# One hybrid decoder layer on one core: attention levels in pairs, output transposes one slot earlier, one input and two row products later

## The chip, the cores and the metric

The kernel runs on one core of one Trainium2 chip. The metric is the device time of one execution in microseconds (us), as the median of several runs; lower is better.

## The reference

One decoder layer in float32 for 256 tokens of width 2048. Cut to what is computed:

```python
mod = silu(c) @ w_ada + b_ada                 # six rows of 2048: sh1 sc1 gt1 sh2 sc2 gt2
h = rmsnorm(x, g_pre_mix) * (1 + sc1) + sh1
proj = h @ w_in                               # GLA q k v r, low-rank gate, MoBA q k v, gates a, b
log_a = log_sigmoid(ga_low @ w_alpha_up + b_alpha) / 16
o_gla = gla(q * dk**-0.5, k, v, log_a)        # 4 heads, causal, decay exp(b_i - b_j), b = cumsum(log_a)
o_gla = rmsnorm(o_gla, g_head) * silu(gr)
o_moba = causal softmax attention of 8 heads  # 256 tokens are one block
merged = sigmoid(gate_a) * (o_gla @ w_gla_out) + sigmoid(gate_b) * (o_moba @ w_moba_out)
x = x + gt1 * rmsnorm(merged @ w_o, g_post_mix)
h = rmsnorm(x, g_pre_ffn) * (1 + sc2) + sh2
u, g = split(causal_conv3(h @ w_up) + b_conv)
x = x + gt2 * rmsnorm((gelu(g) * u) @ w_down, g_post_ffn)
```

## The kernel before, in words

**Slots.** All large weights stream through one ring of four buffers, `raw`, 1 MB each. A piece of weight, numbered w, has a slot of the program. SyncE loads piece w as soon as `used` counts w - 3, that is when TensorE is through with piece w - 4 (`load_grid`, `load_head`, `load_row`, lines 310 to 340 and 370 to 380). ScalarE rounds it into `hi` (`split_hi`, line 488), VectorE subtracts to get the rest, `lo` (`split_lo`, line 868), and TensorE multiplies: 16 matmuls of 512 columns with `hi`, then as many columns' worth with `lo` (helpers from line 1424 on; all their matmuls carry line 1421). ScalarE and VectorE each work three pieces ahead: in the body of slot w they split piece w + 3. Every engine runs its own list of instructions strictly in the order written.

**Stages.** First 33 slots for the two branch gates and the low-rank gate; then four heads of `HEAD_N` = 12 slots; then 16 merge slots; then 16 slots of `w_o`; then the norm and residual, 22 passes of four slots for `w_up` (`up_pass`), and 44 slots for `w_down`.

**A head.** Head I brings one GLA head and two MoBA heads through the slots n = 0 to 11: n = 0, 1 GLA q and k; 2, 3 MoBA q; 4, 5 MoBA k; 6 to 9 both values; 10, 11 the output gate. Attention of the GLA head with its decay is put together from eight levels of masks. For level p, VectorE makes exponents (`level_decay`, two instructions into `eb`), ScalarE takes exp (line 640), VectorE multiplies q and k with them into `Mb` (`level_operands`), TensorE multiplies these (`gram`, one matmul of 128 x 128 in full float32, which the profile shows as two records), and VectorE copies what the level's mask picks out of PSUM into `C` or `A` (`select`). Before the change one level goes through in each of the slots 3 to 10: `gram` is called behind the weights of the slot, and all other steps are spread over the neighbouring slots. `eb` and `Mb` have two buffers, used in turn by even and odd levels.

**Between heads.** Behind slot 11 TensorE forms the head's output (`A` times values, into bank 4). ScalarE squares it and takes a root, VectorE the reciprocal (line 1158). Then, in slot 0 of the next head, ScalarE first splits piece w + 3 and only then scales the output into `ot` (`token_major`, line 592):

```python
                    split_hi(w + 3)
                    if I and n == 0:
                        token_major(I - 1)
                    if I:
                        tail(I - 1, n)
```

TensorE's `tail(prev, n)` does the rest behind the weights of the next head's slots: transposes of the softmax weights `ssb` in slot 0 (line 1601), of `ot` in slot 1 (line 1607; it waits for `ot_done`), the MoBA value products in slot 2. For the last head these lie in the merge slots 0, 0 and 2, and there `token_major` stands ahead of the split.

**Rows of c @ w_ada.** GpSimd loads 128 pieces of 512 KB of `w_ada` (line 474), VectorE accumulates them (`ada_unit`, lines 892, 897), so many in each slot as `UNITS_3`, `UNITS_H`, `UNITS_L` and `UNITS_M` say. The gain row `G1` (`g_post_mix` on all partitions, 1 MB) is loaded by GpSimd behind 96 of them (line 460) once `g_done` counts 2, and multiplied in `w_o` slots 4 and 5 (line 1214).

**Residual.** `x2`, the 2 MB of x for the residual, is loaded by SyncE in the loop over `w_o`, behind the load of piece kt = 4 (line 376); first read by line 747, behind the last split of that stage.

**Sums in the up stage.** In passes 8 and 17 VectorE and ScalarE bring a finished row sum into `asp`, and TensorE adds it up over the partitions with `ones_r`, behind the fourth slot of the same pass, where it waits for `g_lo` (four matmuls of 512 columns). `gate_row` reads the result in the third slot of passes 9 and 18.

Of the kernel before, what the change touches and what calls it, by code (L numbers as in the profile page):

```python
# [12 lines left out]
P = 128  # L13
# [3 lines left out]
def layer_kernel(nc, x, c, w_ada, b_ada, g_pre_mix, w_in, w_alpha_up, b_alpha, g_gla_head, w_gla_out,  # L17
# [70 lines left out]
    UNITS_3 = {25: 1, 26: 1, 27: 1, 28: 2, 29: 2, 30: 2, 31: 2, 32: 1}  # L88
    UNITS_H = [2, 1, 1, 1, 1, 1, 1, 2, 2, 2, 2, 2]
    UNITS_L = [2, 1, 1, 1, 1, 1, 1, 2, 2, 1, 0, 0]  # L90
    UNITS_M = [1, 1, 2, 1, 0, 2, 0, 2, 1, 2, 0, 2, 1, 1, 0, 1]
# [22 lines left out]
    with ctx:  # L114
# [169 lines left out]
        UP_FIRST = (0, 2, 1, 3)  # L284

        def score_cols(qt):
            return slice(0, P) if qt == 0 else slice(P, 3 * P)
# [17 lines left out]
        def _(sp):  # L305
# [65 lines left out]
            for kt in range(KT):  # L371
                sp.wait_ge(used, W_WO + kt - 3)
                load_row(W_WO + kt, wo, kt)
                if kt == 4:
                    sp.wait_ge(oo_ready, 4)
                    sp.dma_start(x2[:, :, :], x_v).then_inc(xr_in, 16)
# [29 lines left out]
        def _(pool):  # L406
# [45 lines left out]
            for u in range(8 * KT):  # L452
                part, t = divmod(u, KT)
                if u == 4 * KT - 2:
                    bias_row(4, acc_a)
                if u == 5 * KT - 2:
                    bias_row(5, acc_b)
                if u == 6 * KT:
                    pool.wait_ge(g_done, 2)
                    pool.dma_start(G1[:, :], g_post_mix[0].partition_broadcast(P)).then_inc(g1_in, 16)  # L460
                if u == 6 * KT + 2:
                    bias_row(6, acc_a)
                    pool.wait_ge(arr[W_UP % 4], fills(W_UP))
                    pool.wait_ge(x2_ready, 6)
                    pool.tensor_copy(hi[:, W_UP % 4, :], raw[:, W_UP % 4, :]).then_inc(hi_done, 1)
                    pool.wait_ge(h2_ready, 8)
                    pool.dma_start(G2[:, :], g_post_ffn[0].partition_broadcast(P)).then_inc(g2_in, 16)
                if u == 7 * KT + 2:
                    bias_row(7, acc_a)
                if u == WIDE_FROM:  # L470
                    pool.wait_ge(tri_done, 1)
                if last_in_slot(u) >= 0:
                    pool.wait_ge(ada_used, last_in_slot(u) + 1)
                pool.dma_start(unit_buffer(u), wada[:, t, PART_COL[part]:PART_COL[part] + 1024]).then_inc(ada_in[unit_slot(u)], 16)  # L474
# [3 lines left out]
        def _(act):  # L478
# [96 lines left out]
            def tail(prev, n):  # L575
                if n == 0:
# [4 lines left out]
                    act.activation(tg[:, :, :], grt[:, :, :], ACT.Tanh, scale=0.5).then_inc(tanh_done, 1)  # L581
                if n == 2:
                    t = om_tile(2 * prev)
# [14 lines left out]
            for I in range(HEADS):  # L598
                for n in range(HEAD_N):
# [32 lines left out]
                    if n in (6, 8):  # L632
                        act.wait_ge(mod_done, 4 + I + 1)
                        for j in range(2 * n - 12, 2 * n - 8):
                            part = ps[:, 6 + j // 4, P * (j % 4):P * (j % 4 + 1)]
                            col = M_SH2 * KT + 8 * I + j
                            act.activation(part, part, ACT.Identity, accum_out=modsf[:, col:col + 1]).then_inc(part_read, 1)
                    for p in ((0, 1) if n == 0 else (n,) if 2 <= n <= 7 else ()):
                        act.wait_ge(e_ready, 8 * I + p + 1)
                        act.activation(eb[:, p % 2, :], eb[:, p % 2, :], ACT.Exp).then_inc(exp_done, 1)  # L640
# [207 lines left out]
        def _(dve):  # L848
# [208 lines left out]
            def before_select(I, lv):  # L1057
                if lv:
                    dve.wait_ge(select_done, 8 * I + lv)
                dve.wait_ge(gram_done, 9 * I + (1 if lv == 0 else lv + 2))  # L1060

            def select(I, lv):
# [4 lines left out]
                if lv == 1:  # L1067
                    dve.wait_ge(a_done, I + 1)
                dve.copy_predicated(C[:, :], mask8[:, lv, :], ps[:, 4 if lv % 2 else 5, 0:P]).then_inc(select_done, 1)
                if lv == 7:  # L1070
# [26 lines left out]
            for I in range(HEADS):  # L1097
                for n in range(HEAD_N):
# [21 lines left out]
                    if n == 2:  # L1120
                        a_zero = link(dve.memset(A[:, 0:3:2, :], 0.0), wait=False)
                    if 3 <= n <= 10:
                        if n == 3:
                            linked(a_zero)
                        before_select(I, max(n - 3, 0))
                        if n - 1 <= 7:
                            level_operands(I, n - 1)
                        if n == 10:
                            dve.wait_ge(p_ready, 4 * I + 4)
                            link(dve.reciprocal(stat[:, 28:32], stat[:, 24:28]), wait=False)  # L1130
                        select(I, n - 3)
                    if 2 <= n <= 7:
                        level_decay(I, n)
                    if n == HEAD_N - 1 and I == HEADS - 1:
# [68 lines left out]
            for kt in range(KT - 3):  # L1203
# [3 lines left out]
                if kt == 2:  # L1207
                    dve.wait_ge(g_done, 1)
                    zero_acc(6)
                if kt in (4, 5):  # L1210
                    cs = slice(1024 * (kt - 4), 1024 * (kt - 3))
                    dve.wait_ge(g_copied, kt - 3)
                    dve.wait_ge(g1_in, 16)
                    dve.tensor_tensor(G1[:, cs], gsum[:, cs], G1[:, cs], ALU.mult).then_inc(g_ready, 1)
                    dve.tensor_copy(ones_r[:, :], ones[:, :])
                if kt == 4:
# [202 lines left out]
        def _(pe):  # L1419
# [158 lines left out]
            def gram(I, p):  # L1578
                bank = 4 if p % 2 else 5
                pe.wait_ge(level_ready, 8 * I + p + 1)  # L1580
                if p == 0:
                    if I:
                        pe.wait_ge(og_f, I)
                    mm(ps[:, 5, 0:P], Mb[:, 0, 0:P], Mb[:, 0, P:]).then_inc(gram_done, 1)
                    return
                if p == 2:
                    pe.wait_ge(a01_done, I + 1)
                else:
                    pe.wait_ge(select_done, 8 * I + max(p - 1, 1))
                mm(ps[:, bank, 0:P], Mb[:, p % 2, 0:P], Mb[:, p % 2, P:]).then_inc(gram_done, 1)  # L1590

# [4 lines left out]
            def tail(prev, n):  # L1596
                if n == 0:
                    for hd in range(2):
# [3 lines left out]
                        ins.then_inc(pt_done, 1)  # L1602
                if n == (1 if prev < HEADS - 1 else 0):
                    pe.wait_ge(ot_done, 2 * prev + 2)
# [3 lines left out]
                    ins.then_inc(ott_done, 1)  # L1608
                if n == 2:
                    for hd in range(2):  # L1610
# [5 lines left out]
            for I in range(HEADS):  # L1616
                for n in range(HEAD_N):
# [18 lines left out]
                    if n == 3:  # L1636
# [4 lines left out]
                        ins.then_inc(gram_done, 1)  # L1641
                    if 3 <= n <= 10:
                        gram(I, n - 3)
                    if n == 5:
                        if I:
# [116 lines left out]
            def up_pass(i, sums=None, order=range(4)):  # L1762
                for p_, n in enumerate(order):
                    g = n // 2
                    if n % 2 == 0:
# [3 lines left out]
                                  None if order == range(4) else h2_is_ready).then_inc(used, 1)  # L1769
                    if sums is not None and n == 3:  # L1770
                        pe.wait_ge(g_lo, sums - 5)
# [6 lines left out]
            up_pass(0, order=UP_FIRST)  # L1778
            with pe.Fori(1, 8) as i:
                up_pass(i)  # L1780
            up_pass(8, 6)
            with pe.Fori(9, 17) as i:
                up_pass(i)
            up_pass(17, 7)
            with pe.Fori(18, UP_ITERS) as i:
                up_pass(i)
# [46 lines left out]
```

## Time and profile before

| | us |
|---|---|
| median of 3 runs | 1461.57 (1461.25 to 1464.21) |
| the profiled execution | 1462.59 |
| its span, first to last instruction | 1460.9 |
| TensorE busy with matmuls | 1428.0 (98%) |
| TensorE busy loading weights | 1215.0 (83%) |
| VectorE busy | 1094.6 (75%) |
| ScalarE busy | 721.0 (49%) |
| chain that ended last | TensorE 86%, VectorE 5%, DMA 4% |

How to read it: matmuls are pipelined, so what a group costs TensorE is the distance from its first start to the first start of the next group, not the duration printed. A timeline row gives the start, the time from the first start to the last end, the engine, the line, the operation, the tiles, the shape, how many instructions are merged, and in brackets the idle time before them and what ended it. Times are from the start of the span.

### The profile page before, as it was taken

The numbers are of one execution on the slowest core, as the hardware profiler recorded it, in microseconds if no ns is written. First come the engines' busy times: TensorE is split into PE (matmuls) and PEld (weight loads), VectorE is DVE, ScalarE is ACT, GpSimd is POOL, SyncE is SP. The second block draws the span as 40 slices with busy tenths as digits, with TensorE's granted clock in tenths as the row PEclk, the third lists the DMA queues.
The fourth block names the chain that finished last, engine by engine and source line by source line (L and its number), as shares of the span: only waits on it lengthen the run. The fifth ranks groups of instructions, "written<-read, shape, count | busy, mean of one in ns | idle before, by whom it ended". The sixth has DMA issues, their size and how long they took to land.

```text
span 1460.9 us, 19754 instructions
## 1 busy us (share of the span) xinstructions
PE 1428.0 (98%) x7322; PEld 1215.0 (83%) x7322; DVE 1094.6 (75%) x1145; ACT 721.0 (49%) x820; POOL 84.6 (6%) x165
## 2 busy tenths in 40 slices
PE   4999999999999999999999999999999999999998
PEld 3788888888888888878888888888888888888886
DVE  6899989898989888845787787777777766545545
ACT  5454354554545466333855554454455455443443
POOL 2000011111111100000000000000000000000000
PEclk9999999999999999999999999999999999999999
DMA  9999979898989877865477776677675655555553
GB/s 361 387 387 385 308 252 371 288 311 277 315 271 299 272 246 250 293 264 201 135 254 239 236 243 222 199 241 239 222 243 174 200 180 195 195 191 189 201 189 128
DMA packets 235833, 367.07 MB, mean 251 GB/s; under 512 B 11503, under 2 KB 161521, under 8 KB 235010
## 3 DMA queue, kind: packets, MB, share of 16 engines
q1 hardware_dynamic: 215840, 294.69, 60.5%
q0 software_dynamic: 18848, 69.23, 13.1%
q10 hardware_dynamic: 1090, 2.40, 0.4%
q8 instruction: 36, 0.59, 0.2%
q14 instruction: 19, 0.16, 0.0%
HBM read 364.18 MB, written 2.10 MB: 251 GB/s over the span
## 4 chain that ended last, share of the span: by engine, by line
PE 86%; DVE 5%; DMA 4%; issue 2%; ACT 2%; SPq 0%; DVEq 0%
PE ps L1421 85%; DVE acc L878 2%; DMA raw<-in_w_in 1%; DMA raw<-in_w_o 1%; DMA adar<-in_w_ada 1%; DVE lo L868 1%; DMA raw<-in_w_up 1%; DMA raw<-in_w_moba_out 1%; ACT hi L488 1%; DVE GA L998 0%; ACT hi L812 0%; DVE lo L1369 0%; DVE yt L1241 0%; PE ps L1671 0%; DVE x L1244 0%
## 5 line engine op out<-in xcount | busy, mean ns | idle before, releaser
L1421 PE MATMUL ps<-hT,hi 128*128 128x512 f32 x1936 | 465.8, 392 | 0.8 <-DVE hT L1266 0.8
L1421 PEld LDWEIGHTS ps<-hT,hi 128*128 128x128 f32 x1936 | 356.1, 188 | 71.6 <-DVE hT L1266 1.1
L488 ACT ACTIVATE hi<-raw 128x2048 fp32r<-128x2048 f32 x115 | 220.3, 1917 | 278.4 <-DMA raw<-in_w_in 190.2
L868 DVE TENSOR_TENSOR lo<-raw,hi 128x2048 fp32r<-128x2048 f32 x115 | 262.7, 2286 | 79.2 <-ACT hi L488 78.9
L1421 PEld LDWEIGHTS ps<-hT,lo 128*128 128x128 f32 x1920 | 246.1, 191 | 9.8 <-DVE lo L868 0.5
L1421 PE MATMUL ps<-hT,lo 128*128 128x256 f32 x1920 | 249.1, 283 | 0.1
L1369 DVE TENSOR_TENSOR lo<-raw,hi 128x2048 fp32r<-128x2048 f32 x88 | 199.2, 2290 | 36.8 <-ACT hi L812 36.6
L1421 PE MATMUL ps<-hi,hT 128*128 128x512 f32 x768 | 186.2, 394 | 0.2 <-DVE GA L998 0.2
L1421 PE MATMUL ps<-hi,asp 128*128 128x512 f32 x704 | 175.8, 389 | 0.0
L812 ACT ACTIVATE hi<-raw 128x2048 fp32r<-128x2048 f32 x88 | 165.8, 1906 | 14.0 <-DMA raw<-in_w_up 12.6
L1421 PEld LDWEIGHTS ps<-hi,hT 128*128 128x128 f32 x768 | 142.5, 188 | 32.3 <-issue 1.4
L1421 PEld LDWEIGHTS ps<-hi,asp 128*128 128x128 f32 x704 | 132.1, 188 | 27.4
L1400 DVE TENSOR_TENSOR lo<-raw,hi 128x2048 fp32r<-128x2048 f32 x40 | 91.7, 2292 | 49.5 <-ACT hi L834 49.5
L474 POOL DMA_DIRECT2D ada<-in_w_ada x128 | 67.7, 530 | 688.5 <-DVE acc_a L1338 295.0
L1421 PE MATMUL ps<-lo,asp 128*128 128x512 f32 x352 | 96.1, 389 | 0.0
L1421 PE MATMUL ps<-lo,hT 128*128 128x512 f32 x384 | 95.0, 389 | 0.0
L790 ACT ACTIVATE cv<-ps 128x512 f32<-128x512 f32 x44 | 26.4, 600 | 125.0 <-PE ps L1421 125.0
L1421 PEld LDWEIGHTS ps<-lo,hT 128*128 128x128 f32 x384 | 72.1, 188 | 15.0
L878 DVE SCALAR_TENSOR_TENSOR acc<-adar,scol,acc 128x1024 f32<-128x1024 f32 x59 | 75.7, 1282 | 11.1 <-DMA adar<-in_w_ada 7.1
L801 ACT ACTIVATE asp<-aT 128x256 fp32r (+1 forms) x44 | 18.0, 416 | 124.7 <-PE ps L1421 124.7
L794 ACT ACTIVATE cv<-up,cols 128x256 f32<-128x256 f32 x88 | 48.2, 595 | 61.5 <-DVE up L1351 61.5
L1421 PEld LDWEIGHTS ps<-lo,asp 128*128 128x128 f32 x352 | 66.0, 188 | 14.0 <-DVE lo L868 0.3
(257 smaller groups left out, 1296.4 us busy)
## 6 DMA issues: line engine op xcount, KB each, us to landing
raw<-in_w_up SPq DMA_DIRECT2D x176, 512.0 KB, 4.5
raw<-in_w_in SPq DMA_DIRECT2D x161, 512.0 KB, 6.0
ada<-in_w_ada POOLq DMA_DIRECT2D x128, 512.0 KB, 5.2
raw<-in_w_down SPq DMA_DIRECT2D x88, 512.0 KB, 4.2
adar<-in_w_ada SPq DMA_DIRECT2D x64, 512.0 KB, 11.0
raw<-in_w_o SPq DMA_DIRECT2D x32, 512.0 KB, 4.9
raw<-in_w_gla_out SPq DMA_DIRECT2D x16, 512.0 KB, 4.9
raw<-in_w_moba_out SPq DMA_DIRECT2D x16, 512.0 KB, 5.8
```

Source lines behind the costliest of these rows:

```text
L474: pool.dma_start(unit_buffer(u), wada[:, t, PART_COL[part]:PART_COL[part] + 1024]).then_inc(ada_in[unit_slot(u)], 16)
L488: act.activation(hi[:, w % 4, :], raw[:, w % 4, :], ACT.Copy).then_inc(hi_done, 1)
L790: act.activation(cv[:, :, :], ps[:, 2 * g:2 * g + 2, TOK:], ACT.Copy).then_inc(cross5, 1)
L794: act.activation(cv[:, ct, :], up[:, ct, 2:], ACT.Identity, scale=cols[:, ds(f + COL_CONV + 4 * FT, 1)], bias=cols[:, ds(f + COL_CB, 1)]). ...
L801: act.activation(asp[:, k, 0:TOK], aT[:, ds(kt, 1), :], ACT.Copy).then_inc(a_hi, 1)
L812: act.activation(hi[:, w % 4, :], raw[:, w % 4, :], ACT.Copy).then_inc(hi_done, 1)
L868: dve.tensor_tensor(lo[:, w % 4, :], raw[:, w % 4, :], hi[:, w % 4, :].bitcast(F32), ALU.subtract).then_inc(lo_done, 1)
L878: ins = dve.scalar_tensor_tensor(a, adar[:, u % 8, :], scol[:, t:t + 1], a, ALU.mult, ALU.add)
L1369: dve.tensor_tensor(lo[:, k, :], raw[:, k, :], hi[:, k, :].bitcast(F32), ALU.subtract).then_inc(lo_done, 1)
L1400: dve.tensor_tensor(lo[:, k, :], raw[:, k, :], hi[:, k, :].bitcast(F32), ALU.subtract).then_inc(lo_done, 1)
L1421: return pe.matmul(out_, lhsT, rhs, start=start, stop=stop)
```

## The change

- Levels in pairs: `gram` is called twice behind each of the slots 3, 5, 7 and 9, and VectorE's selects and operands, and ScalarE's exponentials, go in pairs. `level_place` gives each level of a pair its own columns of PSUM. `UNITS_H` and `UNITS_L` move `ada_unit` calls from slots 3 and 5 to 4 and 6.
- The transposes of `ot` stand in slot 0 of the next head in all heads; the MoBA value products in slot 3.
- `x2` is loaded behind piece kt = 9, `G1` once `used` counts `W_WO + 6`; its product is in `w_o` slots 9 and 10, and `ones_r` is written in slot 2.
- The sums of the up stage stand behind the first slot of passes 9 and 18.

```diff
-    UNITS_H = [2, 1, 1, 1, 1, 1, 1, 2, 2, 2, 2, 2]
-    UNITS_L = [2, 1, 1, 1, 1, 1, 1, 2, 2, 1, 0, 0]
+    UNITS_H = [2, 1, 1, 0, 2, 0, 2, 2, 2, 2, 2, 2]
+    UNITS_L = [2, 1, 1, 0, 2, 0, 2, 2, 2, 1, 0, 0]
...
+        def level_place(p):
+            if p < 2:
+                return (4, slice(2 * P, 3 * P)) if p else (5, slice(0, P))
+            return (4 if p // 2 == 2 else 5), slice(P * (p % 2), P * (p % 2 + 1))
...
-                if kt == 4:
+                if kt == 9:
                     sp.wait_ge(oo_ready, 4)
                     sp.dma_start(x2[:, :, :], x_v).then_inc(xr_in, 16)
...
                 if u == 6 * KT:
-                    pool.wait_ge(g_done, 2)
+                    pool.wait_ge(used, W_WO + 6)
                     pool.dma_start(G1[:, :], g_post_mix[0].partition_broadcast(P)).then_inc(g1_in, 16)
...
-                if n == 2:
+                if n == (3 if prev < HEADS - 1 else 2):
                     t = om_tile(2 * prev)
...
-                    for p in ((0, 1) if n == 0 else (n,) if 2 <= n <= 7 else ()):
+                    for p in ((n, n + 1) if n in (0, 2, 4, 6) else ()):
...
-                    if 3 <= n <= 10:
+                    if n in (3, 5, 7, 9):
                         if n == 3:
                             linked(a_zero)
-                        before_select(I, max(n - 3, 0))
-                        if n - 1 <= 7:
+                        before_select(I, n - 3)
+                        if n < 9:
                             level_operands(I, n - 1)
-                        if n == 10:
-                            dve.wait_ge(p_ready, 4 * I + 4)
-                            link(dve.reciprocal(stat[:, 28:32], stat[:, 24:28]), wait=False)
+                            level_operands(I, n)
                         select(I, n - 3)
-                    if 2 <= n <= 7:
-                        level_decay(I, n)
+                        before_select(I, n - 2)
+                        select(I, n - 2)
+                    if n == 10:
+                        dve.wait_ge(p_ready, 4 * I + 4)
+                        link(dve.reciprocal(stat[:, 28:32], stat[:, 24:28]), wait=False)
+                    if n in (2, 3, 5):
+                        p = {2: 2, 3: 4, 5: 6}[n]
+                        level_decay(I, p)
+                        level_decay(I, p + 1)
...
+                    dve.tensor_copy(ones_r[:, :], ones[:, :])
-                if kt in (4, 5):
-                    cs = slice(1024 * (kt - 4), 1024 * (kt - 3))
-                    dve.wait_ge(g_copied, kt - 3)
+                if kt in (9, 10):
+                    cs = slice(1024 * (kt - 9), 1024 * (kt - 8))
+                    dve.wait_ge(g_copied, kt - 8)
                     dve.wait_ge(g1_in, 16)
                     dve.tensor_tensor(G1[:, cs], gsum[:, cs], G1[:, cs], ALU.mult).then_inc(g_ready, 1)
-                    dve.tensor_copy(ones_r[:, :], ones[:, :])
...
             def gram(I, p):
-                bank = 4 if p % 2 else 5
+                bank, cs = level_place(p)
                 pe.wait_ge(level_ready, 8 * I + p + 1)
...
-                if n == (1 if prev < HEADS - 1 else 0):
+                if n == 0:
                     pe.wait_ge(ot_done, 2 * prev + 2)
...
-                if n == 2:
+                if n == (3 if prev < HEADS - 1 else 2):
                     for hd in range(2):
...
-                    if 3 <= n <= 10:
+                    if n in (3, 5, 7, 9):
                         gram(I, n - 3)
+                        gram(I, n - 2)
...
-                    if sums is not None and n == 3:
+                    if sums is not None and n == 0:
                         pe.wait_ge(g_lo, sums - 5)
...
-            up_pass(8, 6)
+            up_pass(9, 6)
...
-            up_pass(17, 7)
+            up_pass(18, 7)
```

## Rows read from the trace of the kernel before

**Rows 1.** The page, part 1: TensorE's matmuls.

```profile
PE 1428.0 (98%) x7322; PEld 1215.0 (83%) x7322; DVE 1094.6 (75%) x1145; ACT 721.0 (49%) x820; POOL 84.6 (6%) x165
```

**Rows 2.** TensorE's waits: who for whom, us in total, times, longest.

```profile
PE ps L1476 <- DMA rows<-in_b_conv: 16.5, 1, 16.5
```

**Rows 3.** Timeline of TensorE in the w_o stage, kt = 3 to 6.

```profile
637.41 1.98 PE L1421 MATMUL ps<-hi,mT 128*128 128x512 f32 x8
...
650.66 2.11 PE L1421 MATMUL ps<-hi,mT 128*128 128x512 f32 x8 [1.44 <-ACT hi L488]
...
656.75 0.61 PE L1421 MATMUL ps<-hi,mT 128*128 128x512 f32 x2
```

**Rows 4.** The tile x: time from issue to landing of its one load.

```profile
DMA to landing us min/median/max: 13.0/13.0/13.0
```

**Rows 5.** Timeline of TensorE at the end of up pass 8.

```profile
919.84 2.07 PE L1421 MATMUL ps<-hT,lo 128*128 128x256 f32 x16
922.74 1.19 PE L1421 MATMUL ps<-asp,ones_r 128*128 128x512 f32 x4 [0.83 <-DVE asp L1374]
```

**Rows 6.** Timeline of TensorE in head 0: slot 7, and behind slot 9's weights.

```profile
268.63 3.92 PE L1421 MATMUL ps<-hi,hT 128*128 128x512 f32 x16
...
274.34 3.92 PE L1421 MATMUL ps<-hi,hT 128*128 128x512 f32 x16
...
285.63 0.38 PE L1421 MATMUL ps<-Mb 128*128 128x128 f32 x2
285.85 1.48 PE L1421 MATMUL ps<-mqk 128*128 128x128 f32 x8
```

**Rows 7.** Timeline of TensorE in the merge stage: a slot with weights alone.

```profile
605.82 3.79 PE L1421 MATMUL ps<-hi,og_om 128*128 128x512 f32 x16
...
611.26 1.07 PE L1421 MATMUL ps<-hi,og_om 128*128 128x512 f32 x4
```

**Rows 8.** Timeline of TensorE, slot 0 of head 1 to the start of slot 1.

```profile
303.49 2.08 PE L1421 MATMUL ps<-hT,lo 128*128 128x256 f32 x16
305.40 0.82 PE L1601 MATMUL ps<-ident,ssb 128*128 128x128 f32 x6
305.97 3.92 PE L1421 MATMUL ps<-hT,hi 128*128 128x512 f32 x16
```

**Rows 9.** Timeline of ScalarE in the same stretch.

```profile
305.01 1.92 ACT L488 ACTIVATE hi<-raw 128x2048 fp32r<-128x2048 f32 x1 [1.56 <-DMA raw<-in_w_in]
306.83 0.82 ACT L592 ACTIVATE ot<-ps,stat 128x256 f32<-128x256 f32 x2
```

**Rows 10.** Timelines, heads 2 and 3: TensorE's start of slot 1, ScalarE's scaling.

```profile
380.64 3.92 PE L1421 MATMUL ps<-hT,hi 128*128 128x512 f32 x16
...
381.56 0.82 ACT L592 ACTIVATE ot<-ps,stat 128x256 f32<-128x256 f32 x2
...
455.32 3.92 PE L1421 MATMUL ps<-hT,hi 128*128 128x512 f32 x16
...
456.88 0.82 ACT L592 ACTIVATE ot<-ps,stat 128x256 f32<-128x256 f32 x2
```

**Rows 11.** Issues by SyncE, and the split that waited for the second load's landing.

```profile
298.71 0.92 SPq L307 DMA_DIRECT2D raw<-in_w_in  x2
...
656.94 0.81 SPq L307 DMA_DIRECT2D raw<-in_w_o  x2
...
661.75 1.93 ACT L488 ACTIVATE hi<-raw 128x2048 fp32r<-128x2048 f32 x1 [2.57 <-DMA raw<-in_w_o]
```

**Rows 12.** The tile G (instructions), and VectorE's timeline late in the w_o stage.

```profile
L1214 DVE TENSOR_TENSOR G<-gsum,G x2: 1218/1218/1219, 658.9 to 662.7; 128x1024 f32<-128x1024 f32 x2
...
680.50 2.29 DVE L868 TENSOR_TENSOR lo<-raw,hi 128x2048 fp32r<-128x2048 f32 x1 [3.67 <-ACT hi L488]
```

**Rows 13.** Stretches: length, busy time of five engines, granted clock, DMA share, GB/s.

```profile
32.00:40.00 8.00, 8.00 (x31) 5.01 (x32) 6.58 (x13) 3.84 (x5) 0.00 (x0) 0.79 1.05 387
648.00:651.00 3.00, 1.56 (x8) 0.98 (x6) 0.36 (x1) 1.91 (x1) 0.00 (x0) 1.00 1.02 401
```

More of the change, by code:

```diff
@@ L1059, in before_select @@
                     dve.wait_ge(select_done, 8 * I + lv)
-                dve.wait_ge(gram_done, 9 * I + (1 if lv == 0 else lv + 2))
+                dve.wait_ge(gram_done, 9 * I + (lv | 1) + 2)
             def select(I, lv):
@@ L1068, in select @@
                     dve.wait_ge(a_done, I + 1)
-                dve.copy_predicated(C[:, :], mask8[:, lv, :], ps[:, 4 if lv % 2 else 5, 0:P]).then_inc(select_done, 1)
+                bank, cs = level_place(lv)
+                dve.copy_predicated(C[:, :], mask8[:, lv, :], ps[:, bank, cs]).then_inc(select_done, 1)
                 if lv == 7:
@@ L1578, in gram @@
             def gram(I, p):
-                bank = 4 if p % 2 else 5
+                bank, cs = level_place(p)
                 pe.wait_ge(level_ready, 8 * I + p + 1)
[L1581 to L1586, printed above, removed]
+                if p == 0 and I:
+                    pe.wait_ge(og_f, I)
+                if p in (2, 3):
                     pe.wait_ge(a01_done, I + 1)
-                else:
-                    pe.wait_ge(select_done, 8 * I + max(p - 1, 1))
-                mm(ps[:, bank, 0:P], Mb[:, p % 2, 0:P], Mb[:, p % 2, P:]).then_inc(gram_done, 1)
+                if p >= 4:
+                    pe.wait_ge(select_done, 8 * I + (2 if p < 6 else 4))
+                mm(ps[:, bank, cs], Mb[:, p % 2, 0:P], Mb[:, p % 2, P:]).then_inc(gram_done, 1)
             def causal_product(out_, values, weights):
@@ L1778, in _ @@
             up_pass(0, order=UP_FIRST)
-            with pe.Fori(1, 8) as i:
+            with pe.Fori(1, 9) as i:
                 up_pass(i)
-            up_pass(8, 6)
-            with pe.Fori(9, 17) as i:
+            up_pass(9, 6)
+            with pe.Fori(10, 18) as i:
                 up_pass(i)
-            up_pass(17, 7)
-            with pe.Fori(18, UP_ITERS) as i:
+            up_pass(18, 7)
+            with pe.Fori(19, UP_ITERS) as i:
                 up_pass(i)
```

## The prediction

> **What bounds the kernel now.** I began with the page: matmuls keep TensorE busy for 98% of the span [rows 1]. So time can only be won where TensorE stands still or does avoidable work, and the change moves no arithmetic away. Next, TensorE's waits: the largest, 16.5 us, is the start, before any code the diff touches [rows 2]. Then I walked TensorE's timeline and compared starts, since a short stall hides under a "busy" engine. One tile of a w_o slot is 12 matmuls at 0.227 us, 2.72 us. From the first tile of kt = 3 to that of kt = 6 are six tiles, 16.32 us, but the rows say 656.75 - 637.41 = 19.34: 3.0 us are lost there, the longest wait of 1.44 us ending with a ScalarE split that had itself waited for a weight [rows 3]. That is where x comes in, 13.0 us from issue to landing [rows 4]. In up pass 8 the 16 `lo` matmuls should end their turn 1.91 us after 919.84 (the same sixteen take that from 303.49 to 305.40 [rows 8]); the sums start at 922.74, 1.0 us late, waiting for `asp` [rows 5]. In the heads there is no such gap: slots follow each other at full rate.
>
> **Part 1, levels in pairs.** The same 32 levels are multiplied; only their company changes. A slot with one level lasts 274.34 - 268.63 = 5.71 us [rows 6], one with weights alone 611.26 - 605.82 = 5.44 [rows 7]: a lone level costs 0.27. Inside a group of full-float32 matmuls the next start comes 0.22 after it [rows 6]. Dissolving a group into another therefore saves at most 0.05, and not less than nothing. Four groups go per head (slots 4, 6, 8, 10), 16 in all; moving the `ot` transposes and the value products dissolves 3 + 3 more. Eight of the 22 lie ahead of slots shaped like the one measured: 0.4 us. The other fourteen are worth 0 to 0.7; I take 0.2. **Saved 0.6 us, bounds 0.4 to 1.1.**
>
> What the pairs move elsewhere costs nothing as long as its cover holds. VectorE now waits in slot 3 for both levels, with an evacuation and a split queued behind; ScalarE's exponentials of a pair stand behind the split of slots 2, 4 and 6. But splits are three pieces ahead of TensorE, some 17 us at 5.71 a slot, and a pair adds only a few small instructions to VectorE's turn. In slots 4, 6, 8 and 10 it no longer waits for a level at all, which is where the moved `ada_unit` calls go. The sum of the calls is unchanged, as is their number in slots 7 to 11, so GpSimd's loads around the head boundary stay as they are.
>
> **Part 2, output transposes in slot 0.** This is the part that costs. The wait for `ot_done` now stands ahead of all of slot 1's matmuls. Before, TensorE begins slot 1 of head 1 at 305.97, right behind the `ssb` transposes [rows 8]; that is where it would now begin on `ot`. But ScalarE has `ot` ready at 306.83 + 0.82 = 307.65 [rows 9]. Stall: 1.7 us. In head 2: 381.56 + 0.82 - 380.64 = 1.7. In head 3: 456.88 + 0.82 - 455.32 = 2.4 [rows 10]. The last head's transposes already stood in merge slot 0 and do not move. **Sum 5.8 us, all on the path**, as TensorE has nothing else in its queue.
>
> Can ScalarE be earlier? Its scaling stands behind a split that it starts at 305.01, after 1.56 us idle, waiting for the load of piece w + 3 [rows 9]. SyncE could issue that load only when slot 11 was through, 298.71; landing took 6.3 us [rows 11]. The change leaves all of this as it is. The nearest row for a faster landing is a w_o weight with the DMA queues otherwise quiet: issued 656.94, split begun 661.75, 4.8 us [rows 11]. Everything would be 1.5 us earlier, and that is all of ScalarE's idle time (1.56): stalls of 0.2, 0.2 and 0.9, 1.3 in all. For a slower one, the nearest is head 3's own 2.4 in all three heads: 7.1. I take 5.8, since contention at that moment comes from the same neighbours.
>
> **Part 3, x and the post-mix row later.** With no 2 MB of x and no 1 MB row (and no two units behind it in GpSimd's queue) between them, the loads of kt = 4 to 7 come as a quiet load does, 4.8 us, and are split 1.92 later; TensorE wants each over 10 us after its issue. The 3.0 us vanish. They could return later: `used` reaches `W_WO + 6` at about 653.7, and then kt = 9, x, the row and two units are issued together. Taking x at its 13.0 us [rows 4], and half as much again for the 1 MB of kt = 10 behind it in the same queue, that weight lands by 19.5 after the burst, is rounded by 21.4, and TensorE reaches it four slots on, 21.8. So even the slow price fits, by 0.4; a quiet landing (13.0 + 4.8) fits by 2. The row's products, 2 x 1.22 us, now lie in slots 9 and 10, where VectorE idles 3.67 before a split [rows 12]; both results are first read behind this stage. **Saved 3.0 us, bounds 0 and 3.0.**
>
> **Part 4, sums one slot later.** `asp` was 1.0 us late and now has a whole slot more; pass 17 had no such wait. `gate_row` reads two slots later, and VectorE only gets there when TensorE is past the sums. **Saved 1.0 us, bounds 0 and 1.1.**
>
> **Sum:** 5.8 - 0.6 - 3.0 - 1.0 = **+1.2 us** on the profiled execution's own 1462.59. That run was 1.0 above the median of the runs, 1461.57, so on the median's scale I forecast 1461.57 + 1.2 = **1462.8**. No more than 0.2% (2.9 us) can be told from no change here, so this is "same": two repairs of 4 us, eaten by a new wait.
>
> **A rule that speaks against the change.** What rows show first: the one earlier stall of comparable length, at 648 to 651, left the granted clock at 1.00, while from 32 to 40, after a stretch with little matmul work, its mean was 0.79: TensorE was partly at 1.2 GHz, and 8.0 x 0.21 = 1.7 us of work were lost [rows 13]. The Trainium skill (TensorE: Matmul & The Clock Gate, Part 1: The HAM clock gate) has it that an idle TensorE is put back to half rate and has to be busy for a while to get it back. Nothing in the sum rests on it; as a rival it is the second below.
>
> **Rivals.**
> *A, ScalarE arrives sooner* (faster). If the load lands as a quiet one does, stalls shrink to 1.3: -3.3, **1458.3**. For: units were shuffled among the slots. Against: the counts near the boundary are unchanged, and three heads agree within 0.7 us. 12%.
> *B, the clock falls in the new stalls* (slower). Each of three stalls costs another 1.7 of half-rate work: 1.2 + 5.1 = +6.3, **1467.9**. It decides from two heads on (+4.6). By the skill's rule as told above the same would follow wherever a gap counts as idle. Against: the 1.44 us wait with clock 1.00 [rows 3, 13]; for: head 3's is longer. 7%.
> *C, x's stall only moves.* The burst of x, the row and the units is slower than its 13.0 us, and the 3.0 us come back at kt = 10: +4.2, **1465.8**, slower. Against: the margin above. 8%.
> *D, the transposes do not wait*, for instance because work I count as fixed in slot 0 grows anyway: then -4.6, 1457.0. The code excludes it nearly: 2%.
>
> **How the numbers follow.** Forecast case 64%; with its bounds on parts 1 and 2 (+5.8 to between 4.5 and 7.1) it spans 1461.5 to 1464.1, and a median's own scatter some 0.5 more. About 7% is left for things not thought of, mostly slower. Faster by over 0.2%: A, D, 0.14. Same: 0.64. Slower: B, C and the rest, 0.22. The range runs from 1459.0 to 1466.0: it takes in C and the weaker part of A, and leaves out B and the end of A.
>
> **What would show it.** In the changed profile: TensorE idle 1.7, 1.7 and 2.4 us ahead of the `ot` transposes in heads 1 to 3, released by ScalarE's scaling, with clock 1.00; w_o tiles 2.72 apart from kt = 3 to 11, x still landing before the stage ends; no wait on `asp`; eight lone level groups gone in favour of pairs, a pair's slot some 0.45 us over a bare one. I am wrong if that idle is missing or twice as long, or if w_o stalls near kt = 10.

## The result and the profile after

| | us |
|---|---|
| before, median of 16 runs | 1461.74 (1460.52 to 1464.21) |
| changed, median of 16 runs | 1467.05 (1463.19 to 1475.36) |
| ratio | 1.0041, 95% interval 1.0032 to 1.0049 |
| changed, the profiled execution | 1474.32, span 1472.6 |

The change makes the kernel 5.3 us slower, where I had forecast +1.2, called it no change, and given a range of 1459.0 to 1466.0. The profiled execution is one of the slower of its kernel, so its waits are read for their kind and place, and the sizes come from medians.

The page of the changed kernel, part 1, answers [rows 1]: as many matmuls, a longer span.

```profile
PE 1431.5 (97%) x7322; PEld 1219.1 (83%) x7322; DVE 1094.8 (74%) x1144; ACT 720.9 (49%) x820; POOL 83.8 (6%) x165
```

TensorE's waits of the changed kernel. The second line is new; the waits for a `w_o` split and for `asp` of before are gone.

```profile
PE ps L1488 <- DMA rows<-in_b_conv: 16.4, 1, 16.4
PE ps L1616 <- ACT ot L598: 9.6, 3, 3.9
PE ps L1502 <- ACT xn L522: 4.6, 1, 4.6
```

TensorE's timeline at the start of head 1, answering [rows 8]: softmax transposes, the wait, the `ot` transposes (L1616), and then slot 1.

```profile
304.45 2.08 PE L1433 MATMUL ps<-hT,lo 128*128 128x256 f32 x16
306.37 0.81 PE L1610 MATMUL ps<-ident,ssb 128*128 128x128 f32 x6
311.06 1.11 PE L1616 MATMUL ps<-ident,ot 128*128 128x128 f32 x4 [3.88 <-ACT ot L598]
311.83 5.89 PE L1433 MATMUL ps<-hT,hi 128*128 128x512 f32 x16
317.55 1.72 PE L1433 MATMUL ps<-hT,lo 128*128 128x256 f32 x13
```

The place and the releaser are the forecast ones; the size is not. I had read off 1.7 us, here it is 3.9. And the 16 matmuls behind it take 5.89 us where slot 1's took 3.92 before [rows 8].

The bracket prints a little less than TensorE loses. Counted from start to start, the wait is 311.06 - 306.37 - 0.65 = 4.0 us, where 0.65 is what the six softmax transposes take when nothing holds up the next group (305.26 to 305.91 in a run below). In heads 2 and 3 it is 3.1 and 3.0 by the same count, 10.1 in all. Lengths of single waits below are counted in this way; the lines of the waits view print some tenths less.

ScalarE's timeline in the same stretch, answering [rows 9]: its idle time before the split is 3.95 us, not 1.56.

```profile
304.12 0.30 ACT L661 ACTIVATE stat<-stat,eps 128x2 f32<-128x2 f32 x1
308.37 1.91 ACT L494 ACTIVATE hi<-raw 128x2048 fp32r<-128x2048 f32 x1 [3.95 <-DMA raw<-in_w_in]
310.19 0.82 ACT L598 ACTIVATE ot<-ps,stat 128x256 f32<-128x256 f32 x2
```

SyncE's timeline: the load that this split waits for, answering [rows 11]. From its issue to the split it took 308.37 - 299.68 = 8.7 us, against 6.3 before.

```profile
299.68 0.92 SPq L313 DMA_DIRECT2D raw<-in_w_in  x2
```

Stretches of the changed kernel: length, busy time of TensorE's matmuls and weight loads, VectorE, ScalarE, GpSimd, then the granted clock, DMA share, GB/s. The first three each hold the start of one head.

```profile
304.00:322.00 18.00, 14.12 (x73) 12.19 (x72) 12.40 (x19) 8.66 (x14) 2.59 (x5) 0.81 0.83 270
384.00:402.00 18.00, 15.02 (x79) 12.95 (x79) 13.16 (x21) 9.76 (x14) 2.64 (x5) 0.91 0.88 297
463.00:481.00 18.00, 15.21 (x82) 13.23 (x81) 16.08 (x23) 11.23 (x19) 2.11 (x4) 0.91 0.76 246
482.00:1472.00 990.00, 982.14 (x5090) 841.31 (x5088) 685.95 (x685) 490.44 (x526) 34.90 (x63) 1.00 0.65 218
```

Behind all three waits TensorE ran partly at 1.2 instead of 2.4 GHz; from 482 us on it is at full clock. Rival B has happened.

The `w_o` stage, answering [rows 3], from the first tile of kt = 3: tiles 2.72 us apart, no wait.

```profile
653.45 1.98 PE L1433 MATMUL ps<-hi,mT 128*128 128x512 f32 x8
655.26 1.07 PE L1433 MATMUL ps<-lo,mT 128*128 128x512 f32 x4
656.16 1.98 PE L1433 MATMUL ps<-hi,mT 128*128 128x512 f32 x8
```

The load of x now takes 14.2 us, from `DMA to landing us min/median/max: 14.2/14.2/14.2`, 1.2 more than before, and nothing waits for it. The sums of the up stage start 1.91 us after the `lo` group ahead of them, with no wait, answering [rows 5]:

```profile
938.40 2.08 PE L1433 MATMUL ps<-hT,lo 128*128 128x256 f32 x16
940.31 1.09 PE L1433 MATMUL ps<-asp,ones_r 128*128 128x512 f32 x4
```

### The profile page after: what moved, and what is told of

It is laid out like the page before. It is cut to its first block, busy times and chain, and to the rows that moved or that the text cites. A ratio compares the mean times of both kernels' runs of the same rounds, so it can differ in the third digit from the quotient of the medians.

```text
span 1472.6 us, 19749 instructions
## 1 busy us (share of the span) xinstructions
PE 1431.5 (97%) x7322; PEld 1219.1 (83%) x7322; DVE 1094.8 (74%) x1144; ACT 720.9 (49%) x820; POOL 83.8 (6%) x165
## 4 chain that ended last, share of the span: by engine, by line
PE 87%; DMA 5%; DVE 3%; ACT 2%; issue 1%; SPq 1%; DVEq 0%
PE ps L1433 87%; DMA raw<-in_w_in 3%; DVE acc L884 1%; DMA adar<-in_w_ada 1%; ACT hi L494 1%; DMA ada<-in_w_ada 1%; DMA raw<-in_w_moba_out 1%; SPq L313 0%; DVE acc_a L903 0%; DVE lo L874 0%; DVE yt L1253 0%; DVE x L1256 0%; PE ps L1681 0%; PE ps L1616 0%; PE ps L1660 0%
```

## The experiments

All were timed beside the kernel before on the same chip; medians are in us. "Before" was 1461.87, 1462.18, 1461.86 and 1461.96 in the four groups of runs. Sizes of single waits are from one profiled execution each, and single waits differ by 1 us and more between two executions of one kernel.

### What the place of the transposes is worth

**Changed kernel, transposes back in slot 1.**

```diff
-                if n == 0:
+                if n == (1 if prev < HEADS - 1 else 0):
                     pe.wait_ge(ot_done, 2 * prev + 2)
```

> The changed kernel with the output transposes back in slot 1 of the next head. If their wait in slot 0 and the half-rate clock behind it are the whole loss: no wait on ot, granted clock 1.00 in the heads, and the savings of the other parts remain, -4.6 us against the kernel before, about 1457. If the pairs or the moved units disturb VectorE or the loads by themselves: TensorE idles elsewhere in the heads and the time stays at 1461 or above.

Measured: 1458.34, ratio 0.9975 (0.9967 to 0.9984). TensorE's waits have no line for `ot`, and the heads run back to back. So slot 0 costs 1467.05 - 1458.34 = 8.7 us, and the rest of the change saves 3.5, not 4.6. The two medians are from different groups of runs; by the two ratios the price would be 9.6 us, and their intervals allow 7 to 12.

**Kernel before, transposes in slot 0.** The move of the transposes and nothing else.

> The kernel before with the output transposes moved to slot 0 and nothing else. If the loss is this wait alone and it is as long as in the changed kernel (about 10 us in three stalls, plus 1 to 2 us each of half rate): +10 us or more against before, about 1471. If the changed kernel's stalls are longer than the 5.8 us that I read off because the pairs and units delay the load: stalls of about 1.7, 1.7 and 2.4 us here, +6 us, about 1468, and little or no half rate.

Measured: 1468.81, ratio 1.0053 (1.0036 to 1.0069), 6.9 us slower. The profiled execution, 1466.09, is the fastest of its six; its waits are short and its clock in the heads is full:

```profile
PE ps L1607 <- ACT ot L592: 3.9, 3, 1.8
```

The move alone makes the kernel slower. By starts the three waits are 1.2, 2.0 and 1.2 us, 4.4 in all, and this execution is 4.2 above the median of before, 1461.87: waiting accounts for it. The median of 6.9 is nearer to the second theory (+6) than to the first (+10 or more). It is 1.1 above the 5.8 that I had read off, and the six runs have a mean granted clock of 0.9973, where the runs of before in this group have 0.9985: so some half rate seems to occur here too.

### What makes ot late

**Changed kernel, ScalarE scales before it splits.**

```diff
-                    split_hi(w + 3)
                     if I and n == 0:
                         token_major(I - 1)
+                    split_hi(w + 3)
```

> The changed kernel with ScalarE's scaling of ot put ahead of its split of piece w + 3 in slot 0, in all heads. The transposes stay in slot 0. If the stall is the order on ScalarE (scaling behind a split that waits for a load): stalls fall from 3 to 4 us to at most 0.5 us, what is left being VectorE's reciprocal behind its own split; no half rate; about 1458.5. If ot is late for another reason, the stalls stay above 1.5 us.

Measured: 1461.5, ratio 0.999 (0.9982 to 0.9999), 5.6 below the changed kernel. Timeline of head 1, ScalarE and then VectorE: the scaling no longer waits for a load. It waits 2.62 us for the reciprocal, which VectorE makes behind its own split.

```profile
302.97 0.30 ACT L661 ACTIVATE stat<-stat,eps 128x2 f32<-128x2 f32 x1
305.88 0.84 ACT L598 ACTIVATE ot<-ps,stat 128x256 f32<-128x256 f32 x2 [2.62 <-DVE stat L1170]
...
303.49 2.28 DVE L874 TENSOR_TENSOR lo<-raw,hi 128x2048 fp32r<-128x2048 f32 x1
305.69 0.16 DVE L1170 RECIPROCAL stat<-stat 128x2 f32<-128x2 f32 x1
```

The first order explains most of the wait, and a second one lay hidden under it. I had expected at most 0.5 us of it to be left, and 1458.5; that was too little and too fast. TensorE still waits, by starts 0.9, 0.3 and 1.1 us:

```profile
PE ps L1616 <- ACT ot L598: 1.7, 2, 0.9
```

**The same, and VectorE's reciprocal before its split in slot 11.**

```diff
-                    split_lo(w + 3)
                     if n == HEAD_N - 1:
                         dve.wait_ge(root_done, I + 1)
                         dve.reciprocal(stat[:, 14:16], stat[:, 12:14]).then_inc(rr_ready, 1)
+                    split_lo(w + 3)
```

> The changed kernel, transposes in slot 0, with ScalarE's scaling ahead of its split as in the earlier run (1461.5, stalls left of 0.9, 0.3 and 1.1 us that ended with the scaling, which itself waited 2.6 us for VectorE's reciprocal), and now VectorE's reciprocal ahead of its split in slot 11 too. If both orders together made ot late: no stall at slot 0, 1458 to 1459, as with the transposes in slot 1. If something else holds ot up: stalls of 0.3 us or more stay and the time stays near 1461.

Measured: 1458.62, ratio 0.9977 (0.9967 to 0.9986). Head 1, TensorE, then ScalarE and VectorE:

```profile
305.26 0.81 PE L1610 MATMUL ps<-ident,ssb 128*128 128x128 f32 x6
305.91 0.60 PE L1616 MATMUL ps<-ident,ot 128*128 128x128 f32 x4
...
303.54 0.84 ACT L598 ACTIVATE ot<-ps,stat 128x256 f32<-128x256 f32 x2 [0.23 <-DVE stat L1169]
...
303.34 0.17 DVE L1169 RECIPROCAL stat<-stat 128x2 f32<-128x2 f32 x1 [0.43 <-ACT stat L661]
```

`ot` is ready at 304.38, 1.5 us ahead of its use, and in heads 2 and 3 TensorE does not wait for it either; 0.2 us is left in the merge stage, where the transposes stood in slot 0 before too. With both orders turned the move is free within what these runs tell (1458.62 against 1458.34 in slot 1): the place in slot 0 is not the cause, the two producers behind splits are.

### Why the wait was longer than read off

**Changed kernel, unit counts of before.**

```diff
-    UNITS_H = [2, 1, 1, 0, 2, 0, 2, 2, 2, 2, 2, 2]
+    UNITS_H = [2, 1, 1, 1, 1, 1, 1, 2, 2, 2, 2, 2]
```

(`UNITS_L` likewise.)

> The changed kernel with the unit counts of before in slots 3 to 6 (1, 1, 1, 1 in place of 0, 2, 0, 2). If the moved units are what lengthens the landing at the head boundary (8.3 us for the second half of the load in head 1, against 5.9 before): stalls shrink to the 5.8 us in all that I had read off, about 1463. If it is the pairs' timing on VectorE, or contention that comes out differently from run to run: stalls stay near 10 us and the time near 1467.

Measured: 1465.17, ratio 1.0022 (1.0011 to 1.0033), 1.9 below the changed kernel's first median and 2.4 below its second (next section). The interval just touches that of the first and overlaps that of the second, so the size is uncertain. The waits are 1.4, 2.5 and 3.0 us, 6.9 in all: between the 5.8 and the 10 of the two theories. GpSimd's issues of `w_ada` pieces ahead of the load in question (SyncE, 298.71 before, 299.68 changed, 298.73 in this run): the kernel before, the changed one, and this run.

```profile
294.39 0.53 POOL L474 DMA_DIRECT2D ada<-in_w_ada  x1 [5.49 <-DVE acc_b L897]
295.78 0.53 POOL L474 DMA_DIRECT2D ada<-in_w_ada  x1 [0.86 <-DVE acc_b L897]
```

```profile
296.51 0.53 POOL L480 DMA_DIRECT2D ada<-in_w_ada  x1 [6.30 <-DVE acc_b L903]
297.90 0.53 POOL L480 DMA_DIRECT2D ada<-in_w_ada  x1 [0.86 <-DVE acc_b L903]
```

```profile
294.67 0.53 POOL L480 DMA_DIRECT2D ada<-in_w_ada  x1 [6.30 <-DVE acc_b L903]
296.06 0.53 POOL L480 DMA_DIRECT2D ada<-in_w_ada  x1 [0.86 <-DVE acc_b L903]
```

With the counts changed only in slots 3 to 6, VectorE comes to its units of slot 10 later. In head 1 their buffers come free 1.8 and 3.2 us ahead of the load, where it was 2.9 and 4.3; with the old counts it is 2.7 and 4.1 again. The same two distances can be read at the three head boundaries of twelve profiles, those in which neither order was turned and the counts were one of these two sets:

| kernel | boundaries | first piece ahead of the load, mean us | issue to split, us |
|---|---|---|---|
| old counts, single levels | 12 | 4.0 | 5.8 to 7.5, mean 6.4 |
| old counts, pairs | 6 | 3.7 | 5.4 to 7.6, mean 6.5 |
| the change's counts, pairs | 18 | 2.5 | 6.1 to 8.7, mean 7.3 |

So it is the moved units and not the pairs that make the load late, by about 0.8 us a boundary, 2.5 in three: about what this run takes away. That sharing the DMA engines with the 512 KB pieces is the link is argued from these distances; no run shows it by itself. Old counts are not free of long landings either: 7.6 us in head 3 of this run.

**Changed kernel, no units in slots 10 and 11.** Meant to take those pieces out of the way.

```diff
-    UNITS_H = [2, 1, 1, 0, 2, 0, 2, 2, 2, 2, 2, 2]
+    UNITS_H = [2, 1, 1, 2, 2, 2, 2, 2, 2, 2, 0, 0]
```

> The changed kernel with no units in slots 10 and 11 of heads 0 to 2, and two in each of slots 3 to 6 instead (18 a head as before), so that no piece of w_ada is in flight when the load that ScalarE waits for is issued. If sharing the DMA engines with those pieces is what stretches the landing from 6.5 to between 7.8 and 8.9 us behind the output product: landing in 5 us or a little more, three stalls of about 0.3 to 1 us, little half rate, 1459 to 1461. If the landing is long by itself: unchanged, 1467.

Measured: 1476.49, ratio 1.0097 (1.0082 to 1.0112), a miss in both ways. In heads 1 and 2 it did not empty the DMA engines: two units in each of slots 3 to 9 make VectorE so late that a piece is still issued 0.7 us ahead of the load, and the split begins 7.5 and 8.0 us behind the load's issue. In head 3 no piece is issued in the 5.8 us ahead of it, but ScalarE comes to its split late, at 465.77, without waiting for the load, and VectorE's reciprocal begins only at 467.34. So by the old orders `ot` is late all the same:

```profile
PE ps L1616 <- ACT ot L598: 9.9, 3, 4.0
```

So it does not tell what a quiet landing would be. That figure stays open.

### What the clock adds

**The changed kernel again.**

> The changed kernel itself once more, on the same chip as the three others. Its first profile was one of its slowest executions (1474.32 against a median of 1467.05). Expected: median 1466 to 1468, three stalls between 1.5 and 4 us, and half rate behind those over about 2.5 us only, so that stalls and half rate together account for its scatter.

Measured: 1467.54, ratio 1.0035 (1.0023 to 1.0046). Its profiled execution has waits of 2.3, 2.7 and 3.0 us, and half rate behind all three, also behind the one below the 2.5 that I had expected. The clock in the heads:

```profile
304.00:322.00 18.00, 15.82 (x89) 13.89 (x88) 14.81 (x21) 8.56 (x13) 2.42 (x5) 0.91 0.93 313
384.00:402.00 18.00, 15.48 (x86) 13.50 (x85) 14.96 (x21) 8.57 (x13) 2.11 (x4) 0.91 0.85 291
463.00:481.00 18.00, 15.20 (x76) 12.97 (x75) 13.91 (x20) 8.39 (x12) 1.58 (x3) 0.81 0.73 231
```

18 us at means of 0.91, 0.91 and 0.81 are 1.6 + 1.6 + 3.4 = 6.6 us of work at full rate; some of that time was waiting, in which the clock costs nothing. What it costs can be read from starts. The `ot` transposes and the 16 matmuls behind them take 4.1 us at full rate (305.91 to 310.03 in head 1 with both orders turned) and here 5.8, 5.6 and 7.0: 6.0 us lost. With 8.0 of waiting that makes 14.0, and this execution (1472.41) is 14.1 above the kernel with its transposes in slot 1. In the first profile of the changed kernel it is 10.1 of waiting and 2.4 + 1.7 + 1.3 = 5.4 of half rate (in head 1, 317.55 - 311.06 = 6.5 in place of 4.1), 15.5 for 16.0. The two together are the whole loss in both.

**Six matmuls in the wait.** TensorE multiplies the identity with a constant while it waits.

```diff
                 if n == 0:
+                    if prev < HEADS - 1:
+                        for _k in range(6):
+                            mm(ps[:, 5, :], ident[:, :], causal[:, :])
                     pe.wait_ge(ot_done, 2 * prev + 2)
```

> The changed kernel with six extra matmuls of 512 columns (identity times a constant, 0.43 us each, into a bank that the transposes overwrite) between TensorE's softmax transposes and its wait for ot, in heads 1 to 3. It changes no dependency, only what TensorE does while it waits. If half rate behind the stalls comes from TensorE's idleness: the granted clock stays 1.00 in the heads, no matmuls 0.43 us apart behind the transposes, and where the stall is over 2.6 us nothing is lost by the filler: 1 to 3 us less than the changed kernel, 1464 to 1466. If the clock does not matter, the time is the changed kernel's or up to 1 us more per head with a short stall.

Measured: 1474.78, ratio 1.0081 (1.0068 to 1.0094), where I had expected 1464 to 1466. The filler was twice as long as I wrote:

```profile
307.18 5.32 PE L1433 MATMUL ps<-causal,ident 128*128 128x512 f32 x12
312.33 0.60 PE L1619 MATMUL ps<-ident,ot 128*128 128x128 f32 x4
312.69 1.63 PE L1433 MATMUL ps<-hT,hi 128*128 128x512 f32 x6
```

`ot` was always ready first. Three fillers of 5.2 us on the 1458.34 of transposes in slot 1 make 1474, as measured. The clock is whole, although TensorE was kept from its real work for longer than in the changed kernel:

```profile
304.00:322.00 18.00, 18.00 (x90) 13.66 (x89) 14.06 (x21) 8.96 (x14) 2.64 (x5) 1.00 0.91 294
```

**Three matmuls.** The same with `range(3)`.

> As the six-matmul filler, with three. Each of those matmuls in full float32 turned out as two records of 0.43 us, so six took 5.2 us where the stall was 2.3 to 4; three take 2.6. If idleness is what brings half rate: none behind the transposes, idle of at most 1.4 us left in each head, and where the stall exceeds 2.6 us the filler is free: 3 to 4 us less than the changed kernel's 1467.3, 1463.5 to 1465. If half rate costs nothing by itself, or comes anyway: 1467 or more.

Measured: 1467.52, ratio 1.0038 (1.0024 to 1.0051). The granted clock in the heads is 1.00 again, as expected, but no time is won, where I had expected 3 to 4 us. The filler sets a floor of 2.6 us a head, and its profiled execution waits 0.4 more in one head only; that makes about 8.3, against 8.7 for the changed kernel with its clock. Filling the wait removes the half rate and not the loss. That fits a typical execution that loses mostly by waiting, which is argued here and not shown.

How much the clock costs in a typical execution can be estimated from the 16 runs of the changed kernel. Their mean granted clocks average 0.9971, from 0.993 to 0.999, against 0.998 in the profile of before: 0.0009 x 1465 = 1.3 us. Against the 88 runs of before beside the experiments, which average 0.9983, it is 1.8. The clocks are recorded in steps of 0.001, and they count waiting as well, so this is no more than an estimate. The two slowest runs, 1475.36 and 1474.32, have 0.995 and 0.993.

### The other parts alone

**Before with pairs and their unit counts.** The change's edits to levels and units alone.

> The kernel before with the pairs of levels and their unit counts alone; transposes in slot 1, value products in slot 2, x, the row and the sums as before. By my reading: -0.4 to -0.6 us, about 1461.2, TensorE's single-level slots gone. If pairs cost something (VectorE late, longer landings that reach TensorE): slower than before, with idle on TensorE in the heads.

Measured: 1462.43, ratio 1.0005 (0.9996 to 1.0013): no gain. Lone levels' slots of 5.71 us [rows 6] are gone; in the changed kernel a slot with a pair, and the slot after it, read

```profile
269.79 3.79 PE L1433 MATMUL ps<-hi,hT 128*128 128x512 f32 x16
273.42 1.98 PE L1433 MATMUL ps<-lo,hT 128*128 128x512 f32 x8
275.23 0.60 PE L1433 MATMUL ps<-Mb 128*128 128x128 f32 x4
275.60 3.89 PE L1433 MATMUL ps<-hi,hT 128*128 128x512 f32 x16
279.32 1.98 PE L1433 MATMUL ps<-lo,hT 128*128 128x512 f32 x8
281.13 3.79 PE L1433 MATMUL ps<-hi,hT 128*128 128x512 f32 x16
```

5.81 us, of which the weights take 5.44: the pair costs 0.37 up to the next start, and 0.1 in the slot after, which lasts 5.53. Two lone levels cost 0.54. In the heads some tenths are won. But in this profile (its line numbers are those of the changed kernel) TensorE waits elsewhere for a late ScalarE and VectorE, at the merge stage, which before had neither line:

```profile
PE ps L1616 <- ACT ot L598: 0.8, 1, 0.8
PE ps L1433 <- DVE oo L1095: 0.7, 1, 0.7
```

The wait for `oo` comes and goes: it is in four of the eight profiles that have pairs with the change's counts (0.7 to 1.5 us), and in none of the three that have pairs with the old counts, nor in the four with single levels. So it looks like a price of the moved units and not of the pairs; no run has the change's counts with single levels.

**Before with late x and row.**

```diff
-                if kt == 4:
+                if kt == 9:
                     sp.wait_ge(oo_ready, 4)
...
-                    pool.wait_ge(g_done, 2)
+                    pool.wait_ge(used, W_WO + 6)
```

(and the products in slots 9 and 10.)

> The kernel before with x behind kt = 9, the post-mix row and two units once used counts W_WO + 6, and its products in slots 9 and 10. By my reading: w_o tiles 2.72 us apart from kt = 3 to 11, -3.0 us, about 1458.9. If x's stall only moves: TensorE idle near kt = 10, and the time of before.

Measured: 1458.96, ratio 0.9974 (0.9963 to 0.9984), 2.9 us faster. Tiles are 2.72 us apart through the stage. The wait for a `w_o` split is in all four profiles with x behind kt = 4 (1.3 to 1.7 us at its longest) and in none with x behind kt = 9, so this gain is not one execution's.

**Before with late sums.**

```diff
-                    if sums is not None and n == 3:
+                    if sums is not None and n == 0:
```

(and passes 9 and 18 in place of 8 and 17.)

> The kernel before with the up stage's sums behind the first slot of passes 9 and 18. By my reading: no wait on asp, -1.0 us, about 1460.9. If the wait varies from run to run or is given back elsewhere: within 0.5 us of before.

Measured: 1461.43, ratio 0.9998 (0.9989 to 1.0007), 0.4 us below before. The interval, -1.6 to +1.0 us, holds both nothing and the full 1.0. The traces tell more. The run with pairs alone has the sums in their old place and no wait there:

```profile
920.78 2.08 PE L1433 MATMUL ps<-hT,lo 128*128 128x256 f32 x16
922.69 1.09 PE L1433 MATMUL ps<-asp,ones_r 128*128 128x512 f32 x4
```

Nor have the kernel before with its transposes in slot 0 and the one with late x. Of the four profiles with the sums in their old place only the kernel before waits on `asp`: what I had read off was one execution's.

### Better versions

**Transposes in slot 1, unit counts of before, and the rest of the change.**

> Transposes back in slot 1, and the unit counts of before as well (1, 1, 1, 1 in slots 3 to 6): pairs, late x and row, late sums. If the moved units also cost something where nothing waits for ot: 0.5 to 1 us less than with transposes in slot 1 alone (1458.34), about 1457.5. If units matter only through the wait for ot: the same within 0.5 us.

Measured: 1457.84, ratio 0.9969 (0.9957 to 0.9981), the best of the study: 4.0 us below before, 9.2 below the changed kernel.

**Transposes in slot 0, both orders turned, unit counts of before.**

> The same with the unit counts of before in slots 3 to 6. If slot 0 is as good a place as slot 1 once ot is early: the time of the best run so far, 1457.84, within 0.5 us. If the earlier reciprocal makes VectorE late for splits: TensorE waits on lo, and the time is above 1459.

Measured: 1458.31, ratio 0.9973 (0.9962 to 0.9983). Within 0.5 us of the last, as are the two versions with the change's unit counts (1458.34, 1458.62). Once `ot` is early, the slot of the transposes makes no difference that these runs can tell.

## Why the prediction was wrong

**Part 2, +5.8, was the right mechanism and too small: it measured 8.7.** The price was 6.9 in the kernel before, 7.3 in the changed kernel with the old counts (1465.17 - 1457.84), and 8.7 with the change's own. Two steps failed.
- "GpSimd's loads around the head boundary stay as they are", and in part 2 "The change leaves all of this as it is". I argued from the number of unit calls, which indeed stayed, and not from when VectorE gets to them. It gets there later, so the pieces go out closer to the weight: the load takes 7.3 us on average where it took 6.4. With the old counts, 1.9 to 2.4 us of the loss are gone, of which 0.5 (1458.34 - 1457.84, within noise) may have nothing to do with `ot`. My upper bound of 7.1 took the slowest of three landings of one execution for the slowest there is. The lower bound of 4.5 that the range uses is derived nowhere; the working gives 1.3. And single readings scatter: the three waits make 10.1 us in one profile of the changed kernel and 8.0 in the next.
- Rival B had 7%, and came true in part. I priced it as 1.7 us in each of three heads if it came at all. It comes behind some waits in some executions: an estimated 1.3 to 1.8 us in a typical one, and 5.4 and 6.0 in the two profiled ones, where the waits are long. The 1.44 us row that I held against it was shorter than any of the waits that then did it. Here the rule of the Trainium skill that I had cited (TensorE: Matmul & The Clock Gate, Part 1) agrees with the trace in kind: the clock is lower behind idleness (0.81 to 0.91 means) and whole when the wait is filled (1.00).

**Part 3, -3.0, was right,** in mechanism and size: -2.9 measured, and the margin at kt = 10 held although x took 14.2 us.

**Part 4, -1.0, was too large:** -0.4, which these runs can tell neither from nothing nor from 1.0. One execution's wait was taken for every execution's.

**Part 1, -0.6, was not won:** +0.6, interval about -0.6 to +1.9. Its gain in the heads is small, and "costs nothing as long as its cover holds" was not safe for the stage behind the heads, where VectorE's lateness reaches TensorE in half of the profiles with the change's counts. With an interval this wide, 0.6 is not excluded either.

**The sum:** instead of 5.8 - 4.6 = 1.2 it is 8.7 - 3.5 = 5.2. The forecast of no change failed by the size of part 2 above all (2.9 of the 4.0 us), with the three gains short by 1.1. The measured 1467.05 lies 1.05 above my range.

What I had listed as signs came out as follows: waits ahead of the `ot` transposes released by ScalarE, yes, but "twice as long" in head 1, which I had named as proof against me; clock 1.00, no; `w_o` and `asp`, yes; a pair's slot 0.37 us over its weights, near the 0.45.

## What to carry to other kernels

When an instruction moves ahead of other work on the engine that sets the time, follow its input back through every engine and look at what stands in front of each producer in program order. Here two producers, 0.8 and 0.16 us long, stood behind splits that were not urgent, and turning both orders around made the early place free. Treat the landing of a transfer as a range from several occurrences and executions, and recompute when its neighbours are issued whenever the change moves work of the engine that releases them. A wait of some microseconds on TensorE can cost more than itself: in the two profiled executions of the changed kernel, 10.1 and 8.0 us of waiting brought another 5.4 and 6.0 us of half rate.

## What the runs showed of the hardware

- The length of a wait does not tell by itself whether half rate follows. For `ot`, waits of 2.3, 2.7, 3.0, 3.1, 3.4, 4.0 and 4.2 us were followed by matmuls of 512 columns 0.43 us apart, and one of 2.8 (no units in slots 10 and 11) and one of 2.5 (old unit counts) were not; nor were those of 2.0 us and less.
- Filling a wait with matmuls whose result is thrown away keeps the clock at 1.00 through it. It gave no time here: three such matmuls took 2.6 us in every head, six 5.2, whether or not `ot` was that late.
- A matmul of 512 columns in full float32 shows as two records of 0.43 us and takes 0.86; one in the rounded form takes 0.227. I had expected half of that for the filler.
